# Sparse attention, later tokens: the probabilities scaled by a product with a diagonal matrix, which ScalarE makes, in place of VectorE's scaling ahead of a transposition

## The chip, the cores and the metric

One core of one Trainium2 chip. The metric is the device time of one execution of the whole kernel in microseconds (us). TensorE does the matrix products and transpositions, VectorE and ScalarE the elementwise work, GpSimd some of the elementwise work, and SyncE issues the loads of weights. In the profile they are PE (PEld is its loading of the stationary operand), DVE, ACT, POOL and SP.

## The reference, cut to what matters

Two transformer blocks on 256 tokens of width 1024 in float32. Near the middle stands the sparse attention (NSA). Its head dimension is 64, and it has 12 heads in two groups. Each query has three branches: over compressed keys, over selected blocks of keys, and over a window. With 256 tokens the last two run over all earlier keys, each with keys and values of its own:

```python
s = jnp.einsum('bqghd,bqgnkd->bqghnk', qb, kg) * scale
p = masked_softmax(s.reshape(...), smask.reshape(...))      # exp(s - max) / sum
o_slc = jnp.einsum('bqghm,bqgmd->bqghd', p, vg.reshape(...))
...
o_win = jnp.einsum('bqghk,bkgd->bqghd', masked_softmax(...), vw)
o = o_cmp * gb[..., 0:1] + o_slc * gb[..., 1:2] + o_win * gb[..., 2:3]
```

So for each query (row) and branch the exponentials are divided by their sum and multiplied by a gate. The kernel applies both as one factor for a row of probabilities, `rowinv`.

## The kernel before, in words

Queries come in two tiles of 128 tokens (`tt` 0 and 1). The attention is cut into 18 units. The first six (`tt == 0`) have two heads each with 128 keys, the last twelve (`tt == 1`) one head each with 256 keys. With two branches, a unit always has 512 columns of scores for 128 queries. In what follows unit 6 is the first of the later tokens and unit 17 the last.

A unit goes through these steps:

- **S**, on PE: the scores, three products into one of six PSUM banks (`group_scores`): with the high part of the keys, with the low part, and a bias for the mask.
- On DVE: the negated maxima (`rowmax`, L2771) and their product with a factor (`negmax`, L2213), in `group_maximum`.
- On ACT: two exponentials of 256 columns that also leave their sums (`group_exponentials`, L1558, the tile `probs`, of which there are three).
- On DVE: in `group_scaled` the reciprocal of the sums (L2788), its product with the gates (`rowinv`), and the scaling of `probs` by `rowinv`: for later units two operations of 256 columns (L2217).
- **T**, on PE: four transpositions of 128x128 against an identity into another bank (`group_transposed`, L916), so that keys stand on the partitions.
- On ACT a rounded copy of them, `pt_hi` (`group_high_probs`, L1561). On DVE the remainder, `pt_lo` (`group_low_probs`), which frees the bank.
- **O**, on PE: products of `pt_hi` and `pt_lo` with the values, six for one branch of a burst, and a burst covers three units. **C**: nine products of the compressed branch. The results are picked up from `obank` as `act_parts` by ACT and DVE.

Each engine has its own program and keeps its order. It waits only on semaphores. The order is written out by hand in loops over steps w:

- PE: S(w+2), then T(w), then C and O where they are due. For later units C is due at w = 7, 8 and 13 and after 17. O of six products is due at 7, 8, 11, 12, 14, 15. O of twelve is due ahead of T(17) and at the end.
- ACT: the exponentials of w, then `pt_hi` of w-2.
- DVE: the maxima of w+1, `group_scaled` of w, then `pt_lo` of w-2.

S(w+2) needs a bank that the exponentials of w-1 have freed, and T(w) one that `pt_lo` of w-3 has freed. After the last O, PE waits for `act_parts` and goes on with the next projection (`out1`) and the MLP, where it is the busy engine.

Of the kernel before, what the change touches and what calls it, by code (L numbers as in the profile page):

```python
# [12 lines left out]
ALU = mybir.AluOpType  # L13
# [157 lines left out]
NSA_UNITS, NSA_BURSTS = group_units()  # L171
# [263 lines left out]
def build(nc, x_in, mem_in, p_in, pos_in, consts_in, weights_in, out):  # L435
    ctx = ExitStack()
    with ctx:
# [5 lines left out]
        def sem(name):  # L443

            if name not in semaphores:
                semaphores[name] = ctx.enter_context(nc.semaphore(name.replace(".", "_")))
            return semaphores[name]

        def flatten(t):
            return t[:, :, :].rearrange("p a b -> p (a b)")  # L450
# [20 lines left out]
        sq = sb("sq", [128, KD, SEQ])  # L471
# [5 lines left out]
        probs = sb("probs", [128, 3, 512])  # L477
# [22 lines left out]
        rowinv = sb("rowinv", [128, 16])  # L500
# [51 lines left out]
        kcat = hid[:, 3072:5120].rearrange("p (h t) -> p h t", h=8)  # L552
        vmla = hid[:, 5120:6144].rearrange("p (a n) -> p a n", a=2)
        lat = hid[:, 6144:6144 + 768].rearrange("p (a t) -> p a t", a=3)
        cosT = vsw[:, 0, :]
        sinT = vsw[:, 1, :]
        scratch = [memk[:, i, j, :] for i in range(2) for j in range(2)] + [memv[:, 0, 0, :]]
# [17 lines left out]
        def const(name, a=0, n=None):  # L575
            at, width = CONST_AT[name]
            return C[:, at + a:at + (width if n is None else a + n)]
# [89 lines left out]
        def bcast(ap, n):  # L667

            return ap.unsqueeze(2).to_broadcast([ap.shape[0], ap.shape[1], n])
# [25 lines left out]
        block = ctx.enter_context(nc.Block())  # L695
# [43 lines left out]
        def _(pe):  # L739
# [174 lines left out]
            def transpose(dst, src):  # L914
                k = src.shape[0]
                return nc.tensor.transpose(dst, src, const("ident")[0:k, 0:k])  # L916
# [116 lines left out]
            def group_transposed(n):  # L1033
                dst = take("nsa", "T", n)
                if n < 4:
                    keep_busy(dst, 8 if n == 0 else 3)
                pe.wait_ge(sem("nsa.scaled"), n + 1)
                for i in range(4):
                    last = transpose(dst[:, 128 * i:128 * i + 128], probs[:, n % 3, 128 * i:128 * i + 128])
                ready(last)  # L1040

            def begin_outputs(burst):
# [116 lines left out]
            dst = take("mem.sums", 0)  # L1159
            for k in range(KD):  # L1160
                j = k % 4
                last = mm(dst[32 * j:32 * j + 32, 0:SEQ], const("ones", 0, 32), sq[:, k, :], k < 4, k >= 4)
# [3 lines left out]
            dst = take("mem.stat", 0)  # L1166
            for tt in range(TT):
                last = mm(dst[:, tt:tt + 1], square_sum[:, 128 * tt:128 * tt + 128], const("ones", 0, 1))
# [29 lines left out]
            dst = take("ln.mean", 0)  # L1198
            for c in range(CONV_TILES):
# [4 lines left out]
                last = mm(dst[:, 0:SEQ], const("ones"), conv[:, c, :], c == 0, c == CONV_TILES - 1)  # L1204
# [8 lines left out]
            dst = take("ln.var", 0)  # L1213
            for c in range(CONV_TILES):
                pe.wait_ge(sem("ln.squares"), c + 1)
                last = mm(dst[:, 0:SEQ], const("ones"), sq[:, c, :], c == 0, c == CONV_TILES - 1)
# [7 lines left out]
            for t in range(ahead):  # L1224
                w, _ = split_tile("out0", t)
                dst = take("out0", t)
# [4 lines left out]
            for t in range(ahead):  # L1231
                w, _ = split_tile("out0", t)
                for k in range(CONV_TILES):
                    if t == 0:
                        pe.wait_ge(sem("mixed0.act"), k + 1)
                    last = half_products(bank("out0", t), w, k, act_parts, False, k == CONV_TILES - 1)
# [88 lines left out]
            dst = take("kc", 0)  # L1325
            w2k = const("w2_k").rearrange("p (k c) -> p k c", k=2)
            for k in range(2):
                last = mm(dst[:, 0:32], w2k[:, k, :], cmph[:, 0, k, :], k == 0, k == 1)
# [5 lines left out]
            dst = take("gates", 0)  # L1334
            for k in range(KD):
                last = product(dst[0:36, 0:SEQ], [part[:, k, :] for part in gate_weights], [part[:, k, :] for part in projected],
                               k == 0, k == KD - 1)
            ready(last)
            pe.wait_ge(sem("kc.squares"), 1)
            dst = take("kc.norm", 0)  # L1340
# [3 lines left out]
            dst = take("gates.T", 0)  # L1344
            for tt in range(TT):
                last = transpose(dst[:, 36 * tt:36 * tt + 36], slots[0:36, 3, 128 * tt:128 * tt + 128])
# [4 lines left out]
            dst = take("vc", 0)  # L1351
            for g in range(2):
                for k in range(2):
                    last = mm(dst[0:96, 64 * g:64 * g + 64], cmph6[:, k, g, :, :].rearrange("p j n -> p (j n)"), w2v[:, k, :],
                              k == 0, k == 1)
# [85 lines left out]
            dst = take("krope.swap", 0)  # L1441
# [12 lines left out]
            w = block_ready("kv_up")  # L1454
# [45 lines left out]
            for tt in range(TT):  # L1500
                pe.wait_ge(sem("mla.o"), tt + 1)
                dst = take("mla.oT", tt)
                for i in range(4):
                    last = transpose(dst[:, 128 * i:128 * i + 128], otok[:, tt, 128 * i:128 * i + 128])
# [27 lines left out]
            w, _ = split_tile("ple_gate", 3)  # L1532
            dst = take("ple_gate", 3)
            for k in range(KD):
                if k == 4:
                    full_bcast("plegate")
                last = product(dst[:, 0:SEQ], [part[:, k, :] for part in w], [part[:, k, :] for part in projected],
                               k == 0, k == KD - 1)
# [9 lines left out]
        def _(act):  # L1548
# [354 lines left out]
            def group_high_probs(n):  # L1903

                wait_tile(act, "nsa", "T", n)
                if n >= PT_RING:
                    act.wait_ge(sem("nsa.outputs"), sum(burst.covered[0] <= n - PT_RING for burst in NSA_BURSTS))
                slot = n % PT_RING
                high(pt_parts[0][:, 512 * slot:512 * slot + 512], bank("nsa", "T", n)[:, :], "nsa.high_probs")

            def group_high_outputs(burst):

                act.wait_ge(sem("nsa.outputs"), NSA_BURSTS.index(burst) + 1)
                high(act_hi[:, 3 * burst.g:3 * burst.g + 3, 128 * burst.tt:128 * burst.tt + 128],
                     obank(("nsa", burst.tt, burst.g))[:, 0:384].rearrange("p (j t) -> p j t", j=3), "nsa.high_outputs")

            for w in range(len(NSA_UNITS) + 4):
                if w < len(NSA_UNITS):
                    group_exponentials(w)
                if 2 <= w < len(NSA_UNITS) + 2:  # L1920
                    group_high_probs(w - 2)
                if w == 1:
                    act.wait_ge(sem("vbd"), 2)
                    high(vbd_parts[0][0:96, :, :], vbd[0:96, :, :], "nsa.high_compressed_values")
                if w in (2, 3):
                    pump("b_in", 4 + w)
                if w == CMP_TRANSPOSED - 2:
                    act.wait_ge(sem("cmp.centered"), 1)
                    do(flat(cmpp), flat(cmpp), ACT.Exp).then_inc(sem("cmp.probs"), 1)
                if w == CMP_TRANSPOSED + 1:  # L1930
                    wait_tile(act, "cmp.T", 0)
                    high(flat(cmppT_parts[0][0:96, :, :]), bank("cmp.T", 0)[0:96, :], "nsa.high_cmp_probs")
                for burst in NSA_BURSTS:
                    if burst.last and burst.outputs_at == w:
                        group_high_outputs(burst)
# [263 lines left out]
        def _(dve):  # L2199
# [6 lines left out]
            def settle(ins=None):  # L2206

                if ins is not None:
                    step(ins)
                dve.wait_ge(sem("vector_step"), own[0])  # L2210

            def tt_(dst, a, b, op):
                return nc.vector.tensor_tensor(dst, a, b, op)  # L2213

            def ts(dst, a, s, op, s2=None, op2=None):
                if op2 is None:
                    return nc.vector.tensor_scalar(dst, a, s, None, op)  # L2217
                return nc.vector.tensor_scalar(dst, a, s, s2, op, op2)
# [266 lines left out]
            for c in range(CONV_TILES):  # L2485
                ins = stt(conv2[:, c, :], bank("ln.mean", 0)[:, 0:SEQ], -1.0 / 768, conv[:, c, :], ALU.mult, ALU.add)
# [94 lines left out]
            for t in range(4):  # L2581
                dst = tkv[:, t, 0:SEQ] if t < 2 else ksraw[:, t - 2, :]
# [199 lines left out]
            def group_scaled(n):  # L2782

                u = NSA_UNITS[n]
                c, m = STAT_COL["nsa", n], len(u.heads)
                wait_emptied(dve, "nsa", "S", n)
                inv = rowinv[:, 4 * (n % 4):4 * (n % 4) + m]
                settle(nc.vector.reciprocal(inv, rowsum[:, c:c + m]))  # L2788
                f, one = first_head(u)
                own_gates = gate_tok[:, u.tt, :].rearrange("p (h b) -> p h b", b=3)[:, f:f + one:2, 1:3]  # L2790
                pairs = inv.rearrange("p (h b) -> p h b", b=2)
                settle(tt_(pairs, pairs, own_gates, ALU.mult))
                if m == 4:
                    both = probs[:, n % 3, :].rearrange("p (h k) -> p h k", h=m)
                    tt_(both, both, bcast(inv, u.keys), ALU.mult).then_inc(sem("nsa.scaled"), 1)
                    return
                for i in range(m):
                    part = probs[:, n % 3, u.keys * i:u.keys * (i + 1)]
                    last = ts(part, part, inv[:, i:i + 1], ALU.mult)
                last.then_inc(sem("nsa.scaled"), 1)  # L2800

            def group_low_probs(n):

# [284 lines left out]
            for n in range(len(UP_CHUNKS) + 1):  # L3088
# [13 lines left out]
                if n >= 1:  # L3102
                    for t in range(KD * (n - 1), KD * n):
                        wait_tile(dve, "down", t)
                        dst = y[:, t % KD, :]
# [207 lines left out]
```

## Time and profile before

| | |
|---|---|
| median of 3 runs | 1042.76 us (1042.37 to 1043.85) |
| the profiled execution: its time, its span | 1043.11 us, 1041.3 us |
| mean granted clock of TensorE | 0.984 |
| PE, PEld busy | 991.1 us (95%), 887.9 us (85%) |
| DVE busy | 782.3 us (75%) |
| ACT busy | 610.1 us (59%) |
| POOL busy | 192.5 us (18%) |

PE's 95% is an average over the whole kernel. The stretch that the change touches is short, and there the shares are others. Matmul records overlap: each lasts longer than the distance to the next start, so what a row of n records costs PE is the distance between starts, not the sum of durations. The same holds in part for DVE and ACT. This distance is called pitch below.

### The profile page before, as it was taken

What the parts mean: (1) busy time and instruction counts of PE and PEld (TensorE: products, weight loads), DVE (VectorE), ACT (ScalarE), POOL (GpSimd) and SP (SyncE); (2) the same over time, 40 slices, a digit from 0 to 9 for tenths busy, and PEclk for the clock granted to TensorE, in tenths of its full rate; (3) what the DMA queues carried; (4) which work ended last, traced back from release to release, by engine and by line L of the source; (5) the groups of instructions that cost most, each with busy time, mean ns of one, the idle gap of its engine ahead of it and who ended that gap; (6) DMA issues with size and microseconds to landing.
All of it is one profiled execution on the core that took longest, in us unless ns stands there. A gap on an engine that the chain in (4) does not pass through costs nothing.

```text
span 1041.3 us, 17724 instructions
## 1 busy us (share of the span) xinstructions
PE 991.1 (95%) x6807; PEld 887.9 (85%) x6807; DVE 782.3 (75%) x1461; ACT 610.1 (59%) x1143; POOL 192.5 (18%) x99
## 2 busy tenths in 40 slices
PE   4999999999999997899999999998999999999997
PEld 4978888888889986688878888898789999999876
DVE  4788789867868858877987677676566778767786
ACT  5744557564646767646647464565456565645465
POOL 2953112212111001001121121222000000101201
PEclk9999999999999998999999999998999899999999
DMA  9481254554545440034455545422403355554421
GB/s 380 171 241 47 76 203 163 202 194 171 202 162 203 166 164 1 1 122 162 176 194 196 202 167 193 168 92 82 161 3 141 143 192 178 198 184 170 174 79 42
DMA packets 24995, 160.49 MB, mean 154 GB/s; under 512 B 2768, under 2 KB 5072, under 8 KB 6608
## 3 DMA queue, kind: packets, MB, share of 16 engines
q1 hardware_dynamic: 24048, 155.69, 41.8%
q10 hardware_dynamic: 864, 3.66, 0.9%
q8 instruction: 55, 0.90, 0.3%
q14 instruction: 28, 0.23, 0.1%
HBM read 157.86 MB, written 1.49 MB: 153 GB/s over the span
## 4 chain that ended last, share of the span: by engine, by line
PE 79%; DVE 14%; ACT 3%; issue 3%; DMA 1%; POOLq 0%; DVEq 0%; ACTq 0%
PE bank L753 75%; DVE split_lo L624 2%; PE obank L753 2%; PE bank L916 1%; DVE x L2213 1%; DVE tmp L2221 1%; DVE mlp_parts L2221 1%; DMA consts<-in_consts 1%; ACT split_hi L616 1%; DVE rowmax L2771 1%; DVE hidden_parts L2213 1%; DVE tmp L2213 1%; DVE act_parts L2213 1%; ACT L1558 0%; DVE probs L2217 0%
## 5 line engine op out<-in xcount | busy, mean ns | idle before, releaser
L616 ACT ACTIVATE split_hi<-ring 128x1024 fp32r<-128x1024 f32 (+1 forms) x280 | 290.0, 1049 | 117.0 <-PE bank L753 116.4
L753 PE MATMUL bank<-act_parts,split_hi 128*128 128x256 f32 (+1 forms) x1632 | 318.0, 292 | 19.0 <-DVE split_lo L624 12.8
L624 POOL TENSOR_TENSOR split_lo<-ring,split_hi 128x1024 fp32r<-128x1024 f32 (+1 forms) x72 | 175.6, 2446 | 714.5 <-ACT split_hi L616 714.4
L753 PEld LDWEIGHTS bank<-act_parts,split_hi 128*128 128x128 f32 x1632 | 256.6, 190 | 29.1 <-issue 20.1
L624 DVE TENSOR_TENSOR split_lo<-ring,split_hi 128x1024 fp32r<-128x1024 f32 (+1 forms) x208 | 253.5, 1228 | 33.9 <-ACT split_hi L616 33.2
L753 PE MATMUL bank<-hidden_parts,split_hi 128*128 128x512 f32 (+1 forms) x816 | 267.1, 379 | 5.4 <-DVE split_lo L624 2.5
L753 PE MATMUL bank<-act_parts,split_lo 128*128 128x256 f32 x880 | 247.9, 282 | 0.0
L753 PE MATMUL bank<-hidden_parts,split_lo 128*128 128x256 f32 x752 | 210.9, 280 | 0.0
L753 PEld LDWEIGHTS bank<-hidden_parts,split_hi 128*128 128x128 f32 x816 | 149.9, 189 | 37.3 <-DVE split_lo L624 3.1
L753 PE MATMUL bank<-mlp_parts,split_hi 128*128 128x512 f32 x512 | 178.8, 392 | 2.1 <-DVE mlp_parts L2221 2.1
L753 PEld LDWEIGHTS bank<-act_parts,split_lo 128*128 128x128 f32 x880 | 167.1, 190 | 0.0
L753 PE MATMUL bank<-mlp_parts,split_lo 128*128 128x256 f32 x512 | 144.3, 282 | 0.0
L753 PEld LDWEIGHTS bank<-hidden_parts,split_lo 128*128 128x128 f32 x752 | 141.7, 188 | 0.0
L753 PEld LDWEIGHTS bank<-mlp_parts,split_hi 128*128 128x128 f32 x512 | 96.1, 188 | 22.9 <-DVE mlp_parts L2221 2.9
L753 PEld LDWEIGHTS bank<-mlp_parts,split_lo 128*128 128x128 f32 x512 | 96.8, 189 | 0.0
L2213 DVE TENSOR_TENSOR x<-x,bank 128x256 f32<-128x256 f32 x160 | 67.0, 419 | 37.8 <-PE bank L753 34.4
L2221 DVE SCALAR_TENSOR_TENSOR tmp<-bank,consts,tmp 128x255 f32<-128x255 f32 (+1 forms) x88 | 39.7, 475 | 30.5 <-ACT tmp L1558 30.3
L2213 DVE TENSOR_TENSOR tmp<-bank,tmp 128x256 f32<-128x256 f32 x64 | 27.0, 421 | 37.9 <-ACT tmp L1561 35.4
L1558 ACT ACTIVATE tmp<-bank,consts 128x256 f32<-128x256 f32 x45 | 25.3, 563 | 48.4 <-PE bank L753 48.2
L1558 ACT ACTIVATE tmp<-tmp 128x256 f32<-128x256 f32 x64 | 26.7, 418 | 28.4 <-DVE tmp L2221 26.1
L2213 DVE TENSOR_TENSOR hidden_parts<-tmp,hidden_parts 128x256 fp32r<-128x256 f32 x64 | 41.2, 659 | 0.0
L1558 ACT ACT_TABLE_LOAD x29 | 37.2, 1283 | 4.2 <-issue 3.7
(283 smaller groups left out, 1236.9 us busy)
## 6 DMA issues: line engine op xcount, KB each, us to landing
ring<-in_weights SPq DMA_DIRECT2D x141, 1024.0 KB, 4.8
ring<-in_weights SPq DMA_DIRECT2D x5, 768.0 KB, 4.2
shifted<-conv_rows SPq DMA_DIRECT2D x9, 142.0 KB, 4.7
x<-in_x ACTq DMA_DIRECT2D x1, 1024.0 KB, 7.7
y<-in_mem ACTq DMA_DIRECT2D x1, 1024.0 KB, 9.6
out<-x SPq DMA_DIRECT2D x4, 256.0 KB, 2.8
consts<-in_consts ACTq DMA_DIRECT2D x1, 933.0 KB, 12.8
ring<-in_weights SPq DMA_DIRECT2D x1, 512.0 KB, 3.6
```

Source lines behind the costliest of these rows:

```text
L616: nc.scalar.activation(split_hi[:, w % SPLIT, 0:n], src, ACT.Copy).then_inc(sem("high_parts"), 1)
L624: (nc.vector if engine == "vector" else nc.gpsimd).tensor_tensor(split_lo[:, w % SPLIT, 0:n], src, split_hi[:, w % SPLIT, 0:n].bitcast(F32 ...
L753: return nc.tensor.matmul(dst, lhsT, rhs, start=start, stop=stop)
L916: return nc.tensor.transpose(dst, src, const("ident")[0:k, 0:k])
L1558: return nc.scalar.activation(dst, src, func, bias=bias, scale=scale, **more)
L2213: return nc.vector.tensor_tensor(dst, a, b, op)
L2221: return nc.vector.scalar_tensor_tensor(out=dst, in0=a, scalar=s, in1=b, op0=op0, op1=op1)
L2771: settle(nc.vector.reduce_max(rowmax[:, c:c + m], bank("nsa", "S", n)[:, :].rearrange("p (s k) -> p s k", k=u.keys), X_AXIS, negate=True))
```

## The change

For the twelve later units DVE no longer scales `probs`. It stops after `rowinv`. ACT makes, from the identity in the constants, two diagonal matrices of 128x128 (one for each branch) with `rowinv` on the diagonal, into a part of `sq` with room for four units. PE no longer transposes. It computes an ordinary float32 product of the unscaled `probs` (stationary) with the diagonal matrix (moving), which gives the transposed probabilities already scaled. PE waits for a new semaphore, `nsa.diagonals`, in place of `nsa.scaled`. The six earlier units stay as they are.

```diff
+        inverse_diagonals = flatten(sq)[:, 1024:2048].rearrange("p (s h t) -> p s h t", s=4, h=2)
...
-                pe.wait_ge(sem("nsa.scaled"), n + 1)
+                early = sum(u.tt == 0 for u in NSA_UNITS)
+                if n < early:
+                    pe.wait_ge(sem("nsa.scaled"), n + 1)
+                else:
+                    pe.wait_ge(sem("nsa.diagonals"), n + 1 - early)
                 for i in range(4):
-                    last = transpose(dst[:, 128 * i:128 * i + 128], probs[:, n % 3, 128 * i:128 * i + 128])
+                    part, block = dst[:, 128 * i:128 * i + 128], probs[:, n % 3, 128 * i:128 * i + 128]
+                    if n < early:
+                        last = transpose(part, block)
+                    else:
+                        last = mm(part, block, inverse_diagonals[:, n % 4, i // 2, :])
...
+            def group_diagonals(n):
+
+                act.wait_ge(sem("nsa.scaled"), n + 1)
+                inv = rowinv[:, 4 * (n % 4):4 * (n % 4) + 2]
+                for i in range(2):
+                    last = copy(inverse_diagonals[:, n % 4, i, :], const("ident"), inv[:, i:i + 1])
+                last.then_inc(sem("nsa.diagonals"), 1)
...
                     group_high_probs(w - 2)
+                if w < len(NSA_UNITS) and NSA_UNITS[w].tt == 1:
+                    group_diagonals(w)
...
-                settle(tt_(pairs, pairs, own_gates, ALU.mult))
-                if m == 4:
+                ins = tt_(pairs, pairs, own_gates, ALU.mult)
+                if u.tt == 0:
+                    settle(ins)
                     both = probs[:, n % 3, :].rearrange("p (h k) -> p h k", h=m)
-                    tt_(both, both, bcast(inv, u.keys), ALU.mult).then_inc(sem("nsa.scaled"), 1)
-                    return
-                for i in range(m):
-                    part = probs[:, n % 3, u.keys * i:u.keys * (i + 1)]
-                    last = ts(part, part, inv[:, i:i + 1], ALU.mult)
-                last.then_inc(sem("nsa.scaled"), 1)
+                    ins = tt_(both, both, bcast(inv, u.keys), ALU.mult)
+                ins.then_inc(sem("nsa.scaled"), 1)
```

On DVE, in the steps of two later units that follow each other, these rows stand before the change:

```order
L2771 TENSOR_REDUCE rowmax<-bank 128x2 [waits psum_ready]
L2213 TENSOR_TENSOR negmax<-rowmax,rc 128x2 [waits vector_step]
L2788 RECIPROCAL rowinv<-rowsum 128x2 [waits bank_emptied2]
L2213 TENSOR_TENSOR rowinv<-rowinv,gate_tok 128x2 [waits vector_step]
L2217 TENSOR_SCALAR probs<-probs,rowinv 128x256 [waits vector_step]
L2217 TENSOR_SCALAR probs<-probs,rowinv 128x256
L2213 TENSOR_TENSOR pt_lo<-bank,pt_hi 128x512 [waits nsa_high_probs]
```

In the changed kernel the same place on DVE has:

```order
L2790 TENSOR_REDUCE rowmax<-bank 128x2 [waits psum_ready]
L2232 TENSOR_TENSOR negmax<-rowmax,rc 128x2 [waits vector_step]
L2807 RECIPROCAL rowinv<-rowsum 128x2 [waits bank_emptied2]
L2232 TENSOR_TENSOR rowinv<-rowinv,gate_tok 128x2 [waits vector_step]
L2232 TENSOR_TENSOR pt_lo<-bank,pt_hi 128x512 [waits nsa_high_probs]
```

The two scalings and the wait ahead of them are gone. On ACT, in two steps in the middle of the later units, before:

```order
L1558 ACTIVATE probs,rowsum<-bank4,negmax,rc 128x256 [waits psum_ready,negmax]
L1558 ACTIVATE probs,rowsum<-bank4,negmax,rc 128x256
L1561 ACTIVATE pt_hi<-bank5 128x512 [waits nsa_outputs,psum_ready]
L1558 ACTIVATE probs,rowsum<-bank0,negmax,rc 128x256 [waits psum_ready,negmax]
L1558 ACTIVATE probs,rowsum<-bank0,negmax,rc 128x256
```

and in the changed kernel:

```order
L1567 ACTIVATE probs,rowsum<-bank4,negmax,rc 128x256 [waits psum_ready,negmax]
L1567 ACTIVATE probs,rowsum<-bank4,negmax,rc 128x256
L1570 ACTIVATE pt_hi<-bank5 128x512 [waits nsa_outputs,psum_ready]
L1570 ACTIVATE sq<-consts,rowinv 128x128 [waits nsa_scaled]
L1570 ACTIVATE sq<-consts,rowinv 128x128
L1567 ACTIVATE probs,rowsum<-bank0,negmax,rc 128x256 [waits psum_ready,negmax]
L1567 ACTIVATE probs,rowsum<-bank0,negmax,rc 128x256
```

The two copies (they write the diagonals, in `sq`) and their wait for DVE now stand between `pt_hi` of one unit and the exponentials of the next. On PE nothing moves. In each of the twelve places four rows `MATMUL bank<-consts,probs 128x128` become four rows `MATMUL bank<-sq,probs 128x128`.

## Rows read from the trace of the kernel before

**Rows 1.** Windows: length, busy us of PE, PEld, DVE, ACT, POOL, clock, DMA share, GB/s.

```profile
416.26:451.83 35.57, 28.87 (x176) 24.39 (x175) 30.01 (x86) 20.84 (x61) 0.00 (x0) 0.95 0.05 16
430.50:433.50 3.00, 2.92 (x11) 2.95 (x12) 2.75 (x8) 2.38 (x8) 0.00 (x0) 0.50 0.00 0
```

**Rows 2.** Waits from 416 to 452 us: total us, times, longest.

```profile
PE bank L916 <- DVE probs L2217: 4.6, 4, 1.5
```

**Rows 3.** Timeline of DVE, one unit: start, us, what it was.

```profile
434.25 0.69 DVE L2771 TENSOR_REDUCE rowmax<-bank 128x2 f32<-128x512 f32 x1 [0.90 <-PE bank L753]
...
435.05 0.16 DVE L2788 RECIPROCAL rowinv<-rowsum 128x2 f32<-128x2 f32 x1
435.24 0.16 DVE L2213 TENSOR_TENSOR rowinv<-rowinv,gate_tok 128x2 f32<-128x2 f32 x1
435.44 0.61 DVE L2217 TENSOR_SCALAR probs<-probs,rowinv 128x256 f32<-128x256 f32 x2
435.97 0.68 DVE L2213 TENSOR_TENSOR pt_lo<-bank,pt_hi 128x512 fp32r<-128x512 f32 x1
436.57 0.68 DVE L2771 TENSOR_REDUCE rowmax<-bank 128x2 f32<-128x512 f32 x1
```

**Rows 4.** Timeline of ACT, one unit.

```profile
425.72 0.56 ACT L1558 ACTIVATE probs<-bank,negmax,rc 128x256 f32<-128x256 f32 x1
...
426.71 0.21 ACT L1558 ACTIVATION_READ_ACCUMULATOR probs<-bank,negmax,rc 128x1 f32 x1
426.80 0.60 ACT L1561 ACTIVATE pt_hi<-bank 128x512 fp32r<-128x512 f32 x1
427.28 0.58 ACT L1558 ACTIVATE probs<-bank,negmax,rc 128x256 f32<-128x256 f32 x1
```

**Rows 5.** Timeline of PE, units 6 to 17 and the next projection.

```profile
416.85 0.61 PE L916 MATMUL bank<-consts,probs 128*128 128x128 f32 x4
...
419.53 0.63 PE L916 MATMUL bank<-consts,probs 128*128 128x128 f32 x4 [1.49 <-DVE probs L2217]
...
420.95 0.39 PE L753 MATMUL obank<-pt_hi,value_hi 128*128 128x384 f32 x1
...
422.63 0.60 PE L916 MATMUL bank<-consts,probs 128*128 128x128 f32 x4
...
425.71 0.61 PE L916 MATMUL bank<-consts,probs 128*128 128x128 f32 x4
...
430.58 1.09 PE L916 MATMUL bank<-consts,probs 128*128 128x128 f32 x4 [1.09 <-DVE probs L2217]
...
434.05 0.60 PE L916 MATMUL bank<-consts,probs 128*128 128x128 f32 x4
434.41 0.42 PE L753 MATMUL obank<-pt_hi,value_hi 128*128 128x384 f32 x1
...
435.55 0.40 PE L753 MATMUL bank<-kd_hi,query_stack 128*128 128x512 f32 x1
...
445.94 0.60 PE L916 MATMUL bank<-consts,probs 128*128 128x128 f32 x4
...
451.83 0.47 PE L753 MATMUL bank<-act_parts,split_hi 128*128 128x512 f32 x1 [1.43 <-DVE act_parts L2213]
```

**Rows 6.** Timeline of PE, ordinary float32 products elsewhere in the kernel.

```profile
21.93 0.71 PE L753 MATMUL bank<-consts,rc 128*128 128x128 f32 x4 [0.55 <-DVE rc L2230]
22.40 0.48 PE L753 MATMUL bank<-act_parts,split_hi 128*128 128x256 f32 x2
...
1032.48 1.16 PE L753 MATMUL bank<-consts,rc 128*128 128x128 f32 x8
```

**Rows 7.** ACT, groups by shape: form and count, busy us, mean ns.

```profile
L1558 ACT ACTIVATE sq<-y 128x512 f32<-128x512 f32 x3 | 1.9, 625 | 2.3 <-DVE y L2213 2.3
```

**Rows 8.** Timeline of ACT, two operations in a row.

```profile
1008.30 0.40 ACT L1558 ACTIVATE sq<-x 128x256 f32<-128x256 f32 x1
1008.61 0.49 ACT L1561 ACTIVATE act_parts<-x,consts 128x256 fp32r<-128x256 f32 x1
```

## The prediction, made before the changed kernel ran

> **What bounds the kernel now.** I read the windows first. From the scores of unit 8 to the next projection 35.57 us pass; DVE is busy for 30.01 of them, PE for 28.87 by records that overlap, ACT for 20.84 [rows 1]. Next come the waits: in this stretch PE waits 4.6 us in 4 waits for `probs` as DVE has scaled it [rows 2]. So DVE paces most units. Its timeline shows the round of a unit: from one `rowmax` to the next 434.25 to 436.57, 2.32 us. Of this 0.80 goes to the maxima and `negmax`, 0.19 to the reciprocal, 0.20 to `rowinv` and the wait for its result, 0.53 to the scaling, and 0.60 to `pt_lo` [rows 3]. ACT needs 1.08 us for two exponentials (the last sum is written 1.20 after their start) and 0.48 for `pt_hi`, together 1.56, and it waits for the rest [rows 4].
>
> PE is close behind. Its pitches come from its timeline [rows 5]: T costs 0.36 (434.05 to 434.41), O of six 1.10 to 1.14 (434.41 to 435.55), O and S together 1.68 (420.95 to 422.63), so S costs 0.58. T and C together cost 1.42 (419.53 to 420.95), which makes C 1.03. In the steps from T(7) to T(8) and from T(8) to T(9), PE's own work is 0.36 + 1.03 + 1.10 + 0.58 = 3.07 us. These steps take 3.10 and 3.08: here PE, not DVE, sets the pace already. Once, at 430.5 to 433.5, the granted clock is 0.50, which is 1.2 GHz [rows 1]; before it fell, PE had waited 1.09 us for T(11) [rows 5]. There four transpositions and what follows take up 3.47 us until T(12), where DVE's round is 2.32.
>
> **The change part by part.**
>
> DVE loses the two scalings and the wait ahead of them, twelve times. Its round becomes 0.80 + 0.19 + 0.08 + 0.60 = 1.67 us (0.08, an estimate, is half of the 0.16 that `rowinv` lasts [rows 3], since nothing on DVE waits for its result any more). It no longer paces anything.
>
> ACT gains two copies of 128 columns with a pointer as scale. The trace has none of that size. An operation on 256 columns without such a pointer takes 0.40 us, with one 0.49 [rows 8]. 512 columns take 0.625 against 0.40 for 256 [rows 7, 8], so 128 columns less save 0.11. That gives 0.38 to 0.39 for one. The pitch of 0.31 behind a duration of 0.40 [rows 8] takes off 0.09: a pitch of 0.30, two cost 0.60, and the second is written 0.69 after the first starts. Bounds: nothing hides it, and I take the pitch as no cheaper than 0.20, about twice the 0.11 of the slope, and no dearer than 0.41, that of 256 columns (0.49 + 0.01 less 0.09). ACT's round is then a chain: sums written 1.21 after the exponentials start, DVE's reciprocal and `rowinv` 0.20 + 0.16, twice 0.03 to 0.04 from engine to engine, and 0.60, in all 2.24 us. `pt_hi` lies in the wait for DVE. Queued behind the new wait are the next exponentials. So the old pace of 2.32 gains 0.08 at most for a unit.
>
> PE gains the most. Four transpositions are four records. An ordinary float32 product of 128x128 with a moving operand of 128 columns is two records: at 21.93 two such products show as four records with the next work starting at 22.40, 0.47 us, and at 1032.48 eight records end 1.16 after the first starts, which with 0.27 for the last is a pitch of 0.127 [rows 6]. Four products in T are eight records: 0.94 to 1.02 us of PE, against 0.36. I take 0.96, as the clock is full here as at the first of these rows, and 1.20 from the start to the last result. The lower bound is that a product costs what a transposition does, 0.36.
>
> The Trainium skill speaks against this change: Perfetto Trace Analysis, section Transposes, asks that a logical transposition use the transposition and not an ordinary product. It gives no figure; by that rule the sum has the sign of the one worked out here from the rows, and without it PE would gain nothing.
>
> **The sum.** I work out the distance from one T to the next as the longer of PE's own work and the chain through ACT. Done for the kernel before with the same pitches, this gives T(7) to T(11) within 0.05 us of the rows, so the method holds where the clock does. For the changed kernel, with 0.96 for T:
>
> - T(6) to T(7): ACT's copies for unit 6 come ahead of its next exponentials: 2.60. Now 2.68 (416.85 to 419.53).
> - T(7) to T(8) and T(8) to T(9): 0.96 + 1.03 + 1.10 + 0.58 = 3.67 each. Now 6.18 for both (419.53 to 425.71).
> - T(9) to T(10): ACT starts the exponentials only when it has taken up `act_parts`: 1.21, 0.22 for DVE's late maxima, 0.36, 0.04, 0.69, and 0.15 to PE, 2.68. T(10) to T(11): ACT's round, 2.24. Now 4.87 (425.71 to 430.58).
> - T(11) to T(12): 0.96 + 1.14 + 0.58 = 2.68. Now 3.47 at half clock.
> - T(12) to T(13) 2.68, then 2.57 with C, 2.68, 2.25 by ACT, and T(16) to T(17) with O of twelve 0.96 + 2.20 = 3.16: in all 13.34. Now 11.89 (434.05 to 445.94).
> - T(17) to the projection: its last result comes 0.58 later, and `pt_hi`, `pt_lo`, O, `act_parts` follow one another: 6.47. Now 5.89 (445.94 to 451.83) [rows 5].
>
> In all 2.60 + 7.34 + 4.92 + 2.68 + 13.34 + 6.47 = 37.35 us against 34.98 now, 2.4 us more. I assume the full clock throughout, since PE then has 3.08 us of work from T(9) to T(11) where it had 1.88, and waits only 0.70 ahead of T(11) (2.24 less 0.96 and 0.58) where it waited 1.09. Behind the stretch PE is the busy engine, and weights are loaded ahead, so the loss isn't given back. The profiled execution, 1043.11 us, would become 1045.5; the median shown is 0.35 lower, so 1042.76 + 2.4 gives 1045.1.
>
> **The rivals.**
>
> The product is cheap: T stays at 0.36. Then ACT's round and the old steps of PE decide, and the same sum ends 1.6 us earlier than now: 1041.1. For it speaks that the moving operand has only 128 columns, as in a transposition. Against it stand the two records for each product in two places [rows 6]. The same sum breaks even where T costs 0.67, 0.17 for a product; below that the change isn't slower.
>
> The clock falls in a stretch that PE now paces. A spell of 3.0 us at half clock [rows 1] then costs PE 1.5 us in full, on top of the 2.4: 1046.6. For it: some of PE's waits are left. Against it: of the time from T(9) to T(11) PE's work filled 1.88 of 4.87 us before the clock fell, and fills 3.08 of 4.92 in the changed kernel.
>
> ACT's copies are dearer, 0.41 a pitch and 0.92 for both: the same sum gives 3.5 us more, 1046.3. Against it: the slope between 256 and 512 columns is plain. At 0.20 the sum would give 1.4 us more, 1044.2.
>
> The change of engines hides more than I see: PE runs T ahead of a late O, and the loss lies between 0 and 1.5 us, 1042.8 to 1044.2.
>
> **How the numbers follow.** Forecast (1.5 to 3.2 us slower) 0.60; clock 0.13; dear copies 0.07; a cheap product 0.08; the small loss 0.12. The range 1043.2 to 1047.0 leaves out the cheap product and half of the small loss, and a fall of the clock longer than one spell. Since the two sides hold unlike shares: the likeliest case alone is 1044.3 to 1046.0. A measurement of this kernel can tell about 0.2%, 2.1 us, from no change, and the forecast lies just above it: 0.38 of the 0.60 are slower by more, and with clock and copies 0.58. Within 0.2% lies the rest, 0.38, half of the cheap product among it. For faster by over 0.2% the cheap product would need cheap copies and a full clock too, half of its chance: 0.04.
>
> **What the profile would show.** In the changed kernel's trace: 96 records of `bank<-sq,probs` with a pitch near 0.12 in place of 48; copies into `sq` of 0.39 us each; DVE's round at 1.7 us of work with waits for PE and ACT in it; T(7) to T(9) at 7.3 us; the projection starting near 454.2 with PE's waits for DVE gone; and a granted clock of 1.00 at 430 to 434. The prediction is wrong if the records are 48 at 0.09, if the copies take over 0.5, or if the clock falls once more in this stretch.

## The result and the profile after

The changed kernel takes 1045.15 us (median of 11 runs, 1042.75 to 1045.90) against 1043.59 us for the kernel before on the same chip (11 runs, 1041.84 to 1045.02). The ratio is 1.0018, 95% interval 1.0010 to 1.0025. Timed once more, it was 1.0014, interval 1.0004 to 1.0023. Both intervals lie above 1, so it is slower, by some 0.15 to 0.2%, which is close to the least that can be told from no change. The profiled execution took 1044.71 us with a span of 1042.9 us, where the one before took 1043.11 and 1041.3.

The stretch of the later units in windows, the whole and the part that ran at half clock before (columns as in [rows 1]):

```profile
415.84:453.09 37.25, 32.49 (x223) 28.60 (x223) 23.89 (x63) 28.58 (x85) 0.00 (x0) 1.00 0.05 14
430.50:433.50 3.00, 2.51 (x17) 2.32 (x17) 2.47 (x6) 3.00 (x10) 0.00 (x0) 1.00 0.00 0
```

From the scores of unit 8 to the next projection it is 37.25 us long in place of 35.57 [rows 1]. DVE's busy time fell from 30.01 to 23.89, ACT's rose from 20.84 to 28.58 and PE's from 28.87 to 32.49. At 430.5 to 433.5 the granted clock is now 1.00, which is 2.4 GHz, in place of 0.50, which is 1.2 GHz.

Three of the waits of the stretch (total us, times, longest):

```profile
DVE rowmax L2790 <- PE bank L754: 2.9, 4, 0.8
PE bank L754 <- ACT sq L1570: 2.7, 3, 1.2
ACT sq L1570 <- DVE rowinv L2232: 2.3, 6, 1.0
```

PE no longer waits for DVE's `probs` [rows 2]. It waits in 3 places for ACT's diagonals (written into `sq`), and DVE now waits for PE's scores. The timeline of PE, with every T from unit 6 to 12, T(17) and the next projection:

```profile
416.43 1.06 PE L754 MATMUL bank<-sq,probs 128*128 128x128 f32 x8
...
419.27 1.13 PE L754 MATMUL bank<-sq,probs 128*128 128x128 f32 x8 [1.19 <-ACT sq L1570]
...
422.88 1.06 PE L754 MATMUL bank<-sq,probs 128*128 128x128 f32 x8
423.69 0.31 PE L754 MATMUL obank<-cmppT_hi,vbd_hi 96*128 96x128 f32 x1
...
426.42 1.06 PE L754 MATMUL bank<-sq,probs 128*128 128x128 f32 x8
...
429.05 1.13 PE L754 MATMUL bank<-sq,probs 128*128 128x128 f32 x8 [0.98 <-ACT sq L1570]
429.94 0.48 PE L754 MATMUL bank<-kd_hi,query_stack 128*128 128x512 f32 x1
...
431.26 1.13 PE L754 MATMUL bank<-sq,probs 128*128 128x128 f32 x8 [0.49 <-ACT sq L1570]
...
433.87 1.06 PE L754 MATMUL bank<-sq,probs 128*128 128x128 f32 x8
...
446.75 1.05 PE L754 MATMUL bank<-sq,probs 128*128 128x128 f32 x8
...
453.09 0.47 PE L754 MATMUL bank<-act_parts,split_hi 128*128 128x512 f32 x1 [1.43 <-DVE act_parts L2232]
```

Each T is eight records now. Right behind other work it costs PE 0.81 us (422.88 to 423.69), after a wait 0.89 (429.05 to 429.94). Four transpositions cost 0.36 [rows 5]. The timeline of ACT shows its round, from one unit's diagonals to the next:

```profile
430.43 0.69 ACT L1570 ACTIVATE sq<-consts,rowinv 128x128 f32<-128x128 f32 x2
431.03 0.55 ACT L1567 ACTIVATE probs<-bank,negmax,rc 128x256 f32<-128x256 f32 x1
...
432.02 0.19 ACT L1567 ACTIVATION_READ_ACCUMULATOR probs<-bank,negmax,rc 128x1 f32 x1
432.11 0.58 ACT L1570 ACTIVATE pt_hi<-bank 128x512 fp32r<-128x512 f32 x1
432.64 0.69 ACT L1570 ACTIVATE sq<-consts,rowinv 128x128 f32<-128x128 f32 x2
```

The two copies cost 0.60 us of ACT's time and are written 0.69 after they start. The round is 2.21 us (430.43 to 432.64). On DVE the round's work is short, and a wait for PE stands in it:

```profile
434.07 0.69 DVE L2790 TENSOR_REDUCE rowmax<-bank 128x2 f32<-128x512 f32 x1 [0.65 <-PE bank L754]
...
435.14 0.68 DVE L2232 TENSOR_TENSOR pt_lo<-bank,pt_hi 128x512 fp32r<-128x512 f32 x1
436.60 0.69 DVE L2790 TENSOR_REDUCE rowmax<-bank 128x2 f32<-128x512 f32 x1 [0.78 <-PE bank L754]
```

From `rowmax` to `pt_lo` it is 1.07 us, and with 0.60 for `pt_lo` 1.67, in place of 2.32 [rows 3].

One measure is used for all kernels below, the distance on PE's timeline from the start of T(6) to the start of the next projection. It leaves out what happened ahead of T(6), where the clock also differs from one execution to the next. Before it is 34.98 us (416.85 to 451.83, [rows 5]), with the change 36.66 (416.43 to 453.09): 1.68 us more.

### The profile page after: what moved, and what is told of

It reads as the page before. It is cut to its first block, busy times and chain, and to the rows that moved or that the text cites. A ratio compares the mean times of both kernels' runs of the same rounds, so it can differ in the third digit from the quotient of the medians.

```text
span 1042.9 us, 17820 instructions
## 1 busy us (share of the span) xinstructions
PE 993.2 (95%) x6855; PEld 890.7 (85%) x6855; DVE 777.9 (75%) x1437; ACT 617.1 (59%) x1167; POOL 192.5 (18%) x99
## 4 chain that ended last, share of the span: by engine, by line
PE 80%; DVE 12%; ACT 3%; issue 3%; DMA 1%; POOLq 0%; DVEq 0%; ACTq 0%
PE bank L754 76%; PE obank L754 3%; DVE split_lo L625 2%; PE bank L917 1%; DVE x L2232 1%; DVE tmp L2240 1%; DVE mlp_parts L2240 1%; DMA consts<-in_consts 1%; ACT split_hi L617 1%; DVE hidden_parts L2232 1%; DVE tmp L2232 1%; ACT L1567 0%; ACT probs L1567 0%; DVE decays L2240 0%; DVE sq L2232 0%
```

## The experiments

All ratios are against the kernel before on the same chip. In the diffs, `...` stands for lines left out.

**Transpositions in place of the products.** The copies on ACT and all waits stay. The scaling of the later units is left out of the result.

```diff
-                        last = mm(part, block, inverse_diagonals[:, n % 4, i // 2, :])
+                        last = transpose(part, block)
```

> The changed kernel with PE transposing the unscaled probabilities against the identity, as before, in place of the product with the diagonal; the copies on ACT, their waits and the shorter round of DVE stay. It leaves the scaling of the later units out of the result. Theory A (the loss is PE's own time: a product with a pitch of 0.81 us for four in place of 0.36): the projection behind the attention starts some 2.9 us earlier than in the changed kernel, about 1.5 us earlier than in the kernel before, ratio 0.9985. Theory B (the loss is the copies on ACT, which hold the next exponentials and come late for PE): the time stays that of the changed kernel, ratio 1.0018.

Measured: ratio 0.9997 (0.9987 to 1.0008), below the changed kernel's interval. The distance is 34.63 us (416.54 to 451.17). That is 2.0 less than with the products, where 2.9 were expected. PE's timeline shows what is missing:

```profile
428.21 0.64 PE L917 MATMUL bank<-consts,probs 128*128 128x128 f32 x4 [1.44 <-ACT sq L1570]
...
430.42 1.09 PE L917 MATMUL bank<-consts,probs 128*128 128x128 f32 x4 [0.99 <-ACT sq L1570]
...
433.77 0.60 PE L917 MATMUL bank<-consts,probs 128*128 128x128 f32 x4
436.01 0.63 PE L917 MATMUL bank<-consts,probs 128*128 128x128 f32 x4
```

T(11) to T(12) is 3.35 us where ACT's round is 2.21: the half clock is back at the place where the kernel before has it. T(11) to T(13) takes 5.59 us in this trace, two of ACT's rounds at 2.21 would be 4.4: without the spell, 1.15 us less, the distance would be 33.5. The products cost what theory A says, in distance; the ratio of 0.9985 that it gave missed, because it didn't reckon with this spell. Theory B, that only the copies cost, is refuted.

**Products without copies.** The products multiply by the identity from the constants, and PE waits for `rowinv` on DVE. The scaling of the later units is left out of the result.

```diff
...
-                    pe.wait_ge(sem("nsa.diagonals"), n + 1 - early)
+                pe.wait_ge(sem("nsa.scaled"), n + 1)
...
-                        last = mm(part, block, inverse_diagonals[:, n % 4, i // 2, :])
+                        last = mm(part, block, const("ident"))
...
-                    group_diagonals(w)
```

> The changed kernel with products against the identity from the constants: ACT makes no diagonals and PE waits for rowinv on DVE. It leaves the scaling of the later units out of the result. Theory A (PE alone is to blame): no change against the changed kernel, ratio 1.0018. Theory B (ACT's copies alone): faster than before by all that DVE lost, about 5 us, ratio 0.995. Both together (what the step sums say): 2.6 us less than the changed kernel, 1.2 us less than before, ratio 0.9988.

Measured: ratio 0.9988 (0.9977 to 0.9999). The distance is 33.74 us, 2.9 less than with the copies. So the copies cost as well, and the expectation for both together (0.9988, 2.6 less) is the one that held.

**Neither.** The edit of the run above, with transpositions against the identity in place of the products: no copies and no products, again with the scaling of the later units left out.

> The changed kernel with neither: transpositions against the identity, no copies on ACT, PE waits for rowinv on DVE. It leaves the scaling of the later units out of the result, and shows what the relief of DVE is worth by itself. By the step sums the projection starts at 446.8 in place of 451.8: 5.0 us less than before, ratio 0.9952. If DVE's scaling was hidden behind PE anyway, the ratio is above 0.998.

Measured: ratio 0.9959 (0.9945 to 0.9973). The distance is 29.83 us (418.10 to 447.93), 5.1 less than before. The timeline of PE shows units that follow at 1.7 to 2.1 us:

```profile
427.70 0.63 PE L917 MATMUL bank<-consts,probs 128*128 128x128 f32 x4 [0.71 <-DVE rowinv L2227]
...
429.42 0.63 PE L917 MATMUL bank<-consts,probs 128*128 128x128 f32 x4 [0.49 <-DVE rowinv L2227]
...
431.53 0.61 PE L917 MATMUL bank<-consts,probs 128*128 128x128 f32 x4
```

DVE's scaling was thus no hidden work. Not all of the 5.1 us is its price, though: this trace has a granted clock of 1.00 from 410 to 456 us, and the kernel before loses about 1.0 us to its spell of half clock. From its T(11) at 430.58 [rows 5] to T(13), below, it takes 5.62 us, against 4.64 for two rounds of 2.32:

```profile
436.20 0.63 PE L916 MATMUL bank<-consts,probs 128*128 128x128 f32 x4
```

Without the spell the distance before would be 34.0 (the filled kernel below, with a full clock there, measures 34.00), and the scaling is worth 4.2 us. The ratio, some 4.3 us, agrees.

**Products alone.** The kernel before, with DVE's scaling, but with products against the identity.

```diff
-                    last = transpose(dst[:, 128 * i:128 * i + 128], probs[:, n % 3, 128 * i:128 * i + 128])
+                    part, block = dst[:, 128 * i:128 * i + 128], probs[:, n % 3, 128 * i:128 * i + 128]
+                    last = transpose(part, block) if n < 6 else mm(part, block, const("ident"))
```

> The kernel before with DVE's scaling kept, but products against the identity in place of the transpositions of the later units; the result is the reference's. Theory A: nearly the whole loss of the change, 1.5 us or more over the kernel before (2.3 us by the step sums at full clock, less the 0.9 that the spell of half clock costs before), ratio 1.0014 to 1.0022, and no spell of half clock at 430 us. Theory B: no change, ratio 1.000.

Measured: ratio 1.0017 (1.0002 to 1.0032), the ratio of the whole change. The distance is 36.46 us, with a full clock. The change adds to this kernel only the move from DVE's scaling to ACT's copies, and ends at 36.66: the move gains nothing, and the products are nearly all of the loss. The timeline of PE at T(10) and T(11) shows that it still waits for DVE there:

```profile
429.02 1.13 PE L753 MATMUL bank<-consts,probs 128*128 128x128 f32 x8 [0.91 <-DVE probs L2218]
...
431.34 1.13 PE L753 MATMUL bank<-consts,probs 128*128 128x128 f32 x8 [0.61 <-DVE probs L2218]
```

**Copies alone.** The kernel before with two unused copies of 128 columns on ACT in each later step.

```diff
...
+                if 6 <= w < len(NSA_UNITS):
+                    for i in range(2):
+                        copy(inverse_diagonals[:, w % 4, i, :], const("ident"), const("ones", 0, 1))
```

> The kernel before with two idle copies of 128 columns (the identity scaled by a column of ones, result unused, no wait) on ACT in each step of a later unit; the result is the reference's. If the copies cost by the time they take on ACT, 0.60 us a unit beside a round of 1.56, they fit under DVE's 2.32: no change, ratio 1.000 (at most 1.0003). If they cost whenever they stand in the queue, 0.3 to 0.6 us a unit and a ratio of 1.003 or more. Together with the run without copies this tells whether it is their length or the chain through rowinv that costs.

Measured: ratio 1.0001 (0.9993 to 1.0010). The distance is 35.11 us against 34.98, with the same spell of half clock. The time that the copies take on ACT costs nothing under DVE's round: ACT's own work, 1.56 + 0.60 = 2.16 us a unit, is less than 2.32. This doesn't tell why they cost in the change, as the expectation hoped. There they stand in a chain (the exponentials' sums, DVE's `rowinv`, the copies, the next exponentials), but DVE's round is only 1.67, so that ACT's 2.16 would pace by itself. The measured round of 2.21 lies 0.05 above this sum of its own work. No run tells chain and amount of work apart.

**The clock.** The kernel before, with three products that nobody reads ahead of T(10) and of T(11), where PE waits.

```diff
-                if n < 4:
+                if n < 4 or n in (10, 11):
                     keep_busy(dst, 8 if n == 0 else 3)
```

> The kernel before with three products of 512 columns that nobody reads ahead of T(10) and T(11), where PE waits 1.36 and 1.09 us; the result is the reference's. If the spell of half clock at 430.5 to 433.5 us costs what the step sums say, and more work on PE ahead of it keeps the clock up, the projection starts 0.9 us earlier, ratio 0.9991. If the clock falls anyway, no change.

Measured: in the trace as expected; in the time it can't be seen. The distance is 34.00 us (416.24 to 450.24), 0.98 less, with T(11) to T(12) at 2.40 and full clock:

```profile
429.90 0.66 PE L916 MATMUL bank<-consts,probs 128*128 128x128 f32 x4 [0.42 <-DVE probs L2217]
...
432.30 0.63 PE L916 MATMUL bank<-consts,probs 128*128 128x128 f32 x4
```

The ratio is 0.9999 (0.9988 to 1.0010), and the interval holds both 0.9991 and no change. Timed once more:

> The kernel before with idle products ahead of T(10) and T(11), timed once more. Its trace gained the same 1.0 us at the same place, but its time didn't differ. If the spell of half clock stands in most executions of the kernel before, both this and the run before it show a ratio near 0.999; if it comes and goes from one execution to the next, both scatter around 1.000.

Ratio 0.9996 (0.9984 to 1.0008). The windows of this second execution from 416 us on show where the clock was lost instead:

```profile
416.00:426.00 10.00, 9.05 (x55) 8.02 (x55) 8.22 (x24) 5.38 (x18) 0.00 (x0) 0.85 0.00 0
426.00:436.00 10.00, 8.85 (x53) 6.35 (x53) 9.37 (x30) 7.59 (x23) 0.00 (x0) 1.00 0.01 2
```

The fall is gone at 430 us and stands ahead of 420 us. Spans of the two executions were 1036.8 and 1043.4 us for the same code, with mean clocks of 0.990 and 0.981; the first was the fastest of its 12 runs and the second the slowest of its 11, so neither is typical. At 430 us the spell isn't a chance of one execution: all four traces of kernels with transpositions in every unit, T(10) to T(11) in 2.0 us or more and nothing filled in (before, the transposed one, the copies alone, half on GpSimd) have it there, and neither of the two filled ones. But what is gained there in a trace isn't a gain of the kernel that could be measured.

**Half of the scaling on GpSimd.** DVE scales the first branch, GpSimd, idle in this stretch, the second. PE transposes as before.

```diff
...
+                part = probs[:, n % 3, 256:512]
+                nc.gpsimd.tensor_scalar(part, part, rowinv[:, 4 * (n % 4) + 1:4 * (n % 4) + 2], None, ALU.mult)\
+                    .then_inc(sem("nsa.pool_scaled"), 1)
...
```

> The kernel before with the scaling shared out: for later units DVE scales the first branch and GpSimd, idle in this stretch, the second; PE transposes as before; the result is the reference's. DVE's round becomes about 2.1 in place of 2.32. With 0.6 to 0.8 us for 256 columns on GpSimd the step sums give 0.6 to 1.4 us less at full clock, and 0.9 more off if the clock stays up: ratio 0.998 to 0.9995. Rival: GpSimd and DVE hold each other up, or GpSimd needs over 1 us: ratio 1.000 or above.

Measured: ratio 0.9996 (0.9986 to 1.0006), nothing that can be told from no change. GpSimd's row:

```profile
435.16 1.08 POOL L2190 TENSOR_SCALAR probs<-probs,rowinv 128x256 f32<-128x256 f32 x1 [2.57 <-DVE rowinv L2221]
```

It needs 1.08 us where 0.6 to 0.8 were assumed, and DVE 0.35 for the same. This is the rival's case (over 1 us). DVE's round does fall to 2.05 to 2.09, but T waits for the second half. The distance is 34.53 us with the spell of half clock in it, 0.45 less than before, too little to show in the time.

**The change where PE has room.** Product and diagonals for units 6, 9 and 10 alone, in whose steps PE has no C and no O.

```diff
...
-                    if n < early:
+                    if n not in (6, 9, 10):
                         last = transpose(part, block)
...
-                if w < len(NSA_UNITS) and NSA_UNITS[w].tt == 1:
+                if w in (6, 9, 10):
                     group_diagonals(w)
...
```

> The change for units 6, 9 and 10 alone, in whose steps PE has no C and no O and waits for DVE: product and diagonals there, transposition and DVE's scaling for the other nine; the result is the reference's. If the loss is PE's own time where PE paces, it is gone: the step sums give 0.3 us less than before at full clock, ratio 0.9988 to 1.0000 with the clock's 0.9. If the copies' chain costs wherever it stands, 0.1 to 0.6 us for each of the three, ratio 1.0005 or more.

Measured: ratio 0.9989 (0.9980 to 0.9998). The distance is 33.97 us (416.96 to 450.93). The timeline of PE at T(10) to T(12), the first a product and the others transpositions:

```profile
428.55 1.13 PE L754 MATMUL bank<-sq,probs 128*128 128x128 f32 x8 [0.98 <-ACT sq L1570]
...
430.68 0.63 PE L917 MATMUL bank<-consts,probs 128*128 128x128 f32 x4 [0.41 <-DVE probs L2236]
...
433.00 0.63 PE L917 MATMUL bank<-consts,probs 128*128 128x128 f32 x4
```

T(11) to T(12) is 2.32, at full clock. This kernel and the change itself were timed once more together with the filled one above:

> The change for units 6, 9 and 10 alone, timed once more. Its trace was 1.0 us shorter from T(6) to the projection than that of the kernel before, all of it at the place where that one ran at half clock. If this is a gain of the kernel, ratio 0.9985 to 0.9995 again and a clock of 1.00 from 426 to 436 us. If it was the luck of a few runs, 0.9995 to 1.0005.

> The changed kernel itself once more, on the same chip as the next two. Theory A: ratio 1.0015 to 1.0020 again.

Measured: 0.9984 (0.9974 to 0.9994) for the three units, 1.0014 (1.0004 to 1.0023) for the whole change, just under the 1.0015 expected. The distances repeat to 0.02 us, 33.99 and 36.66. The kernel with three units is faster than both kernels, by 0.11 and 0.16% against the one before. Its steps don't explain this. The step sums promised 0.3 us at full clock, but T(6) to T(11) takes 13.72 us (416.96 to 430.68) where the kernel before takes 13.73 (416.85 to 430.58): T(10) to T(11) gains 0.18, and the two steps T(6) to T(7) and T(9) to T(10) lose 0.16 between them. All of the 1.0 us comes after T(11), from the full clock. The filled kernel has the same full clock there and no gain in time that shows. So what makes the kernel with three units faster stays open.

## Why the prediction was right

The mechanism, the sign and the place were right, and one term, T, was too large. That 1045.1 us was forecast and 1045.15 measured is partly luck. The forecast was 2.4 us on top of a median of 1042.76 from 3 runs; over 11 runs the kernel before had 1043.59, and the loss was 1.56 us between the medians, just above the 1.5 at which the forecast's lower end lay. A loss of more than 0.2% had been given 0.58; it was 0.18 and 0.14%.

The step sums against the trace of the changed kernel, in us:

| from, to | before | forecast | measured |
|---|---|---|---|
| T(6), T(7) | 2.68 | 2.60 | 2.84 |
| T(7), T(9) | 6.18 | 7.34 | 7.15 |
| T(9), T(11) | 4.87 | 4.92 | 4.84 |
| T(11), T(12) | 3.47 (half clock) | 2.68 | 2.61 |
| T(12), T(17) | 11.89 | 13.34 | 12.88 |
| T(17), the projection | 5.89 | 6.47 | 6.34 |
| in all | 34.98 | 37.35 | 36.66 |

The kernels side by side, as distances at full clock (34.98 less 1.0 and 34.63 less 1.15 for their spells, the others as measured):

| the scaling of later units | transpositions | products |
|---|---|---|
| on DVE | 34.0 | 36.5 |
| by ACT's copies | 33.5 | 36.7 |
| left out | 29.8 | 33.7 |

Point by point:

- **What bounds.** DVE's round of 2.32 us did pace the units, and work off it was worth 4.2 us at full clock when nothing took its place. PE was already at its own work in the steps of units 7 and 8: with 0.45 us more for each T, T(7) to T(9) went from 6.18 to 7.15 us (419.27 to 426.42), the sum of PE's pitches with 0.81 and 0.89 for T.
- **DVE.** Its round became 1.67 us, as worked out.
- **ACT.** Two copies 0.60, written after 0.69, and a round of 2.21 against 2.24: right to 0.03. That this round gains next to nothing on 2.32 is what took DVE's relief away: of the 4.2 us the copies give back 3.7. Whether the chain or ACT's own 2.16 us of work sets the round isn't shown. One wait was missed, in T(6) to T(7), which was forecast 0.24 too short. ACT's copy of the compressed branch (`cmppT_hi`) now stands behind unit 6's diagonals, and DVE waits for it ahead of the next maxima and of unit 7's `rowinv`, in the changed kernel:

```profile
416.04 0.57 ACT L1570 ACTIVATE cmppT_hi<-bank 96x512 fp32r<-96x512 f32 x1
416.64 0.69 DVE L2232 TENSOR_TENSOR cmppT_lo<-bank,cmppT_hi 96x512 fp32r<-96x512 f32 x1 [0.64 <-ACT cmppT_hi L1570]
```

- **PE, the mis-sized term.** T was taken as 0.96 from the rows of other products [rows 6]. It measured 0.81 in a queue and 0.89 after a wait. The rows weren't unlike T; they were read wrongly. In both, as in T, the records start 0.11 us apart. But both stand behind a wait (at 1032.48 it is the loading of the stationary operand that waited), and there the first record takes longer. These are first records alone: the two of [rows 6], in the kernel before, then a T in a queue and one behind a wait, in the changed kernel:

```profile
21.93 0.38 PE L753 MATMUL bank<-consts,rc 128*128 128x128 f32 x1 [0.55 <-DVE rc L2230]
1032.48 0.38 PE L753 MATMUL bank<-consts,rc 128*128 128x128 f32 x1
...
422.88 0.28 PE L754 MATMUL bank<-sq,probs 128*128 128x128 f32 x1
...
429.05 0.35 PE L754 MATMUL bank<-sq,probs 128*128 128x128 f32 x1 [0.98 <-ACT sq L1570]
```

  Taking 0.47 twice counted the slow start twice, and 1.16 less 0.27, divided by seven, spread it over all records. Over the steps that PE paces, the term makes up the 0.7 us by which the sum overstated. The two other misses, 0.24 too little at T(6) and 0.2 too much at T(9) to T(11) and at the end, cancel.
- **The products' own cost.** On top of DVE's scaling they add 2.5 us, on top of ACT's copies 3.2, and with no scaling 3.9: the less the other engines hold PE up, the more of the products shows. The Trainium skill's rule (Perfetto Trace Analysis, section Transposes), to use the transposition and not an ordinary product, is borne out: 0.36 against 0.81 for four.
- **The clock.** It stayed full, as assumed, and that hid 1.0 us of the loss in these two executions: at full clock for both it is 2.7. The prediction's sign for it set a wait of 0.70 us ahead of T(11) against 1.09 before; the first is by pitches and the second by records. By records it is 0.49 against 1.09, so the reading leans the right way. The rival by which it falls in the changed kernel didn't come in either of its two traces; the trace with transpositions at the same pace had it. The filled kernel shows that with the spell gone at 430 us the clock can fall elsewhere, so I can't say that the products prevent it, only that no trace with products in all twelve units has one between 416 and 452 us (four traces).
- **The rivals.** A cheap product is refuted by the 96 records and the 0.81 us for T, where 0.67 was the price at which the sum broke even. The kernel with transpositions and copies is that rival built, and ends 1.5 us before 34.98 at full clock, where 1.6 was worked out. Dearer copies are refuted by 0.69 for two. The small loss (0 to 1.5 us) is nearly what the time showed: 1.56 us between the medians, where 2.4 were forecast.

## What to carry to other kernels

Moving work off the engine that paces gains only up to the next engine's round. Work out that round with the moved work in it before moving: two copies cost nothing on ACT while DVE took 2.32 us a unit, and nearly as much as DVE's scaling once DVE took 1.67 and ACT 2.21. A multiplication folded into a transposition isn't free in float32: each transposition is one record and each product two. Decide step by step whether such a fold fits, and expect little: in the three steps where PE had room it cost nothing and gained nothing at full clock. And when a price is read off a row that stands behind a wait, take the start off once before multiplying.

## What the runs showed of the hardware

- Four float32 transpositions of 128x128 cost PE 0.36 us, four products of the same shape 0.81 (four and eight records, 0.11 us from start to start in both). Behind a wait the products take 0.89.
- An ACT copy of 128x128 from SBUF with a pointer as scale takes 0.39 us and 0.30 of the engine.
- GpSimd's multiplication of 128x256 by a column takes 1.08 us, three times DVE's 0.35; a plain cast of 128x256 float32 on GpSimd takes 0.50 (six of them, elsewhere in the kernel before).
- The filled kernel had no half clock between 410 and 456 us in one execution and a spell of about 3 us ahead of 420 in another: the same code ran with spans of 1036.8 and 1043.4 us.
